# Late norms, a stationary-weight router and fill-in products in a two-block transformer kernel

## Chip, cores and metric

One core of a Trainium2 chip runs the whole kernel. The metric is the device time of one execution in microseconds (us).

## What is computed

The reference runs two blocks, one after the other, on 256 tokens of width 1024, in float32:

```
x = first_block(x, c, ...)      # 2 layers: h = rms(x)*g*(1+scale)+shift; mixer; x += g1*mix
                                #   layer 0 mixer: forgetting attention (16 heads, causal, cumulative log gates)
                                #   layer 1 mixer: latent attention (rank 768 queries, rank 256 keys and values)
                                #   each layer: x += g2 * grouped_moe(h)  (16 experts, router, best group, top 2)
x = second_block(x, ...)        # 4 layers: x += mixer(rms(x)*w); x += relu(rms(x)*w @ up)**2 @ down
                                #   mixers: retention, MoBA, differential attention, retention
# retention: q, k rotated; s = (q k^T) * decay; o = s v; o = o * rsqrt(mean(o*o) + eps); out = (silu(g) * o) @ w_out
# router: scores = sigmoid(h @ router_w)
```

The shift, scale and gate rows come from silu(c) @ w_mod (6 x 1024 columns a layer). MoBA and the differential layer add a bias that depends on the distance of key and query and is looked up in a table of 32 buckets for each head.

## The kernel before

The 256 tokens are two blocks of 128 (TB = 2); x, [128, 2, 1024], stays on the chip. Each weight is read once, in chunks of 2 MB that are two **pieces** of 1 MB. For accuracy every product is made of three: each operand is split into a high part (float32r) and a low part (the rest), and high x high, low x high and high x low are summed in PSUM. So a piece passes through four hands: SP loads it into one of three `raw` buffers in two transfers of 512 KB (line 773; it waits until VectorE has freed the buffer, line 763), ScalarE copies it to `w_high` in two halves (line 1512, which waits until TensorE is done with the piece three before, line 1508), VectorE subtracts to make `w_low` (line 1885), and TensorE multiplies. ScalarE and VectorE take pieces in program order by `feed(n)`, which stands by hand between their other work. The order on every engine is fixed by the program; semaphores order the engines.

PSUM has two pair buffers of [128, 1024] that all products take in turn (`Use`, by the parity of its number) and Y, [128, 2048], for sums over chunks. A product into a pair waits until the use two before it was emptied (`wait_free`).

**norm** (lines 1043, 1550, 1952). In the early form ScalarE squares and sums x, GpSimd makes 1/rms (lines 845 and 847), VectorE scales x to xn (line 1949), TensorE turns xn round (16 transposes, line 1039), ScalarE writes hT_high and VectorE hT_low. In the **late** form, which mlp and the two softmax layers have, TensorE turns x itself round as soon as it is updated, and 1/rms is applied to the output of the product. The two retentions, the two experts stages, the first norm and the latent norms are early.

**Start of the program.** After the first four shift and scale columns, `thin_product` makes the 16 gate logits of attention A (48 matmuls with hT as the stationary operand and 16 moving columns, lines 968 to 970), then six chunks of `a_proj` follow (`token_product`). Between them TensorE makes running sums (`cum`, lines 1410 and 1421) that ScalarE turns into the biases bias0 and bias1. The table for MoBA's bias is made here too: its inputs are loaded by SP in `needed_later`, TensorE makes it behind `a_proj[0]` (line 1428), VectorE copies it (line 2376), and ScalarE's queue writes it 128 times over to `rel_scratch` in HBM (3 MB, line 1782); it comes back with line 1851 when retention 0 is done. POOL's queue loads w_mod pieces meanwhile (line 829), VectorE sums them by rows (`mod_rows`, lines 1906 and 1909), TensorE makes columns of them behind the last a_proj (`a_mods`, line 978), and GpSimd adds the causal mask to the two biases (line 860).

**experts** (line 1195): norm, router logits by `thin_product`, sigmoid, 13 short VectorE operations to the chosen group (`here`, line 2086), `place_tokens` (ranks), the order of the groups, from which SP takes the addresses of its first expert load, `gather_tokens`, then 16 experts.

**retention** (line 1343): twelve chunks of projections (q, k, v, g), then for each of four heads `scores`, VectorE's decay product (`start`), `weigh`, ScalarE's squares, GpSimd's 1/rms and VectorE's `finish`; when all four are finished, four groups of eight transposes, then four chunks of w_out (lines 1017 to 1027).

## Time and profile before

| | us |
|---|---|
| median of 3 runs (lowest, highest) | 2863.92 (2862.45, 2864.7) |
| the profiled execution, its own time | 2860.61 |
| its span in the trace | 2858.6 |
| TensorE busy | 2522.9 (88%) |
| VectorE busy | 1691.9 (59%) |
| ScalarE busy | 1310.5 (46%) |
| GpSimd busy | 107.3 (4%) |
| mean granted TensorE clock, of full | 0.943 |

PE is TensorE, PEld its weight loads, DVE VectorE, ACT ScalarE, POOL GpSimd, SP the engine that issues most loads; a name with a small q is an engine's queue. The engines run side by side, so the shares do not add up. The order of the stages in the trace, by their starts on TensorE: first products 57.7, attention A 173, experts of layer 0 257, latent layer 708, experts of layer 1 927, retention 0 1362, mlp 0 1586, and then MoBA, mlp, differential attention, mlp, retention 1 and mlp to the end.

### The profile page before, as it was taken

What the parts mean: (1) busy time and instruction counts of PE and PEld (TensorE: products, weight loads), DVE (VectorE), ACT (ScalarE), POOL (GpSimd) and SP (SyncE); (2) the same over time, 40 slices, a digit from 0 to 9 for tenths busy, and PEclk for the clock granted to TensorE, in tenths of its full rate; (3) what the DMA queues carried; (4) which work ended last, traced back from release to release, by engine and by line L of the source; (5) the groups of instructions that cost most, each with busy time, mean ns of one, the idle gap of its engine ahead of it and who ended that gap; (6) DMA issues with size and microseconds to landing.
All of it is one profiled execution on the core that took longest, in us unless ns stands there. A gap on an engine that the chain in (4) does not pass through costs nothing.

```text
span 2858.6 us, 32694 instructions
## 1 busy us (share of the span) xinstructions
PE 2522.9 (88%) x13386; PEld 2163.3 (76%) x13386; DVE 1691.9 (59%) x1455; ACT 1310.5 (46%) x1748; POOL 107.3 (4%) x121
## 2 busy tenths in 40 slices
PE   4876999898667799998998999889997799998999
PEld 4666777786556677776886898679976699886898
DVE  5565788786555777775643555645457455643554
ACT  2351777533333566563343444444444344343443
POOL 1020000010000000000000000100000000000000
PEclk9887999999779899999899999999999999998999
DMA  7821899993431588794453555415543255462553
GB/s 266 235 74 35 287 339 333 348 323 133 166 111 64 180 307 308 269 338 150 146 193 105 197 191 177 162 60 191 190 149 118 82 192 191 153 201 98 172 188 133
DMA packets 231302, 539.89 MB, mean 189 GB/s; under 512 B 21073, under 2 KB 29809, under 8 KB 231153
## 3 DMA queue, kind: packets, MB, share of 16 engines
q1 hardware_dynamic: 209760, 471.99, 48.2%
...
q14 instruction: 44, 0.35, 0.0%
...
## 4 chain that ended last, share of the span: by engine, by line
PE 59%; DVE 18%; DMA 10%; ACT 7%; issue 3%; POOL 1%; SPq 1%; ACTq 0%; DVEq 0%
DVE w_low L1885 7%; PE pair L921 5%; PE pair L923 5%; PE pair L929 5%; PE Y L1017 5%; PE Y L1019 5%; PE Y L1027 5%; DMA raw<-in_exp_w_down 4%; ACT w_high L1512 4%; PE pair L951 3%; PE pair L952 3%; PE pair L957 3%; DMA raw<-in_exp_w_gate 3%; DVE gates L1909 2%; PE Y L1254 2%
## 5 line engine op out<-in xcount | busy, mean ns | idle before, releaser
L1885 DVE TENSOR_TENSOR w_low<-raw,w_high 128x2048 fp32r<-128x2048 f32 (+3 forms) x456 | 1033.5, 2272 | 711.9 <-ACT w_high L1512 707.4
L1512 ACT ACTIVATE w_high<-raw 128x1024 fp32r<-128x1024 f32 (+3 forms) x912 | 911.9, 1039 | 847.6 <-PE Y L1027 237.4
L921 PE MATMUL pair<-hT_high,w_high 128*128 128x256 f32 x1280 | 314.8, 286 | 13.5 <-DVE hT_low L1941 13.5
L923 PE MATMUL pair<-hT_low,w_high 128*128 128x256 f32 x1280 | 314.3, 285 | 0.0
L951 PE MATMUL pair<-w_high,hT_high 128*128 128x512 f32 (+2 forms) x644 | 256.7, 400 | 29.8 <-DVE hT_low L1966 10.7
L921 PEld LDWEIGHTS pair<-hT_high,w_high 128*128 128x128 f32 x1280 | 248.5, 194 | 16.0 <-DVE hT_low L1941 15.1
L952 PE MATMUL pair<-w_high,hT_low 128*128 128x512 f32 (+2 forms) x644 | 254.9, 397 | 0.0
L923 PEld LDWEIGHTS pair<-hT_low,w_high 128*128 128x128 f32 x1280 | 248.6, 194 | 0.9
L1019 PE MATMUL Y<-w_high,gated_low 128*128 128x512 f32 x528 | 205.8, 390 | 0.0
L1017 PE MATMUL Y<-w_high,gated_high 128*128 128x512 f32 x528 | 205.7, 390 | 0.0
L1254 PE MATMUL Y<-w_high,gated_high 128*128 128x512 f32 x320 | 134.5, 420 | 44.6 <-DVE gated_low L2179 39.7
L951 PEld LDWEIGHTS pair<-w_high,hT_high 128*128 128x128 f32 x644 | 126.5, 196 | 57.8 <-DVE hT_low L1941 11.4
L929 PE MATMUL pair<-hT_high,w_low 128*128 128x256 f32 x1280 | 166.6, 283 | 0.0
L957 PE MATMUL pair<-w_low,hT_high 128*128 128x512 f32 (+2 forms) x644 | 160.0, 389 | 5.7 <-DVE w_low L1885 5.7
L929 PEld LDWEIGHTS pair<-hT_high,w_low 128*128 128x128 f32 x1280 | 159.3, 192 | 0.0
L1210 PE MATMUL pair<-w_high,rounded 128*128 128x512 f32 x384 | 152.8, 398 | 2.8 <-DVE gated_low L2179 2.8
L1211 PE MATMUL pair<-w_high,rounded 128*128 128x512 f32 x384 | 150.5, 392 | 0.0
L952 PEld LDWEIGHTS pair<-w_high,hT_low 128*128 128x128 f32 x644 | 126.5, 196 | 25.2
L957 PEld LDWEIGHTS pair<-w_low,hT_high 128*128 128x128 f32 x644 | 120.8, 191 | 31.7 <-DVE w_low L1885 7.4
L1039 PE MATMUL pair<-squares,work 128*128 128x128 f32 x348 | 71.2, 388 | 76.7 <-DVE work L1949 30.9
L1256 PE MATMUL Y<-w_high,gated_low 128*128 128x512 f32 x320 | 131.6, 411 | 0.0
L1027 PE MATMUL Y<-w_low,gated_high 128*128 128x512 f32 x528 | 130.4, 389 | 0.0
...
## 6 DMA issues: line engine op xcount, KB each, us to landing
raw<-in_exp_w_gate SPq DMA_DIRECT2D x128, 512.0 KB, 4.8
raw<-in_exp_w_up SPq DMA_DIRECT2D x128, 512.0 KB, 5.0
raw<-in_exp_w_down SPq DMA_DIRECT2D x128, 512.0 KB, 4.8
raw<-in_w_up SPq DMA_DIRECT2D x128, 512.0 KB, 4.5
raw<-in_w_down SPq DMA_DIRECT2D x128, 512.0 KB, 4.3
...
raw<-in_ret_w_in SPq DMA_DIRECT2D x96, 512.0 KB, 4.7
raw<-in_ret_w_out SPq DMA_DIRECT2D x32, 512.0 KB, 4.0
```

What stands on the lines that cost most here:

```text
L921: nc.tensor.matmul(ps[:, f, :], high[:, k, f * P:(f + 1) * P], hT_high[:, kk, :], start=(kk == 0 and f % 2 == 0), stop=False)
L923: nc.tensor.matmul(ps[:, f, :], high[:, k, f * P:(f + 1) * P], hT_low[:, kk, :], start=False, stop=False)
L929: last = nc.tensor.matmul(ps[:, f, :], low[:, k, f * P:(f + 1) * P], hT_high[:, kk, :], start=False, stop=(kk == KD - 1 and f % 2 == 1))
L951: nc.tensor.matmul(ps[:, b, 0:n], hT_high[:, kk, bs], high[:, k, :], start=(kk == 0), stop=False)
L952: nc.tensor.matmul(ps[:, b, 0:n], hT_low[:, kk, bs], high[:, k, :], start=False, stop=False)
L957: last = nc.tensor.matmul(ps[:, b, 0:n], hT_high[:, kk, b * P:(b + 1) * P], low[:, k, :], start=False, stop=(kk == k_blocks - 1))
L1017: nc.tensor.matmul(y, high_in[:, kk, b * P:(b + 1) * P], high[:, k, ns], start=(first and kk == 0), stop=False)
L1019: nc.tensor.matmul(y, low_in[:, kk, b * P:(b + 1) * P], high[:, k, ns], start=False, stop=False)
L1027: last = nc.tensor.matmul(y, high_in[:, kk, b * P:(b + 1) * P], low[:, k, ns], start=False, stop=False)
L1254: nc.tensor.matmul(y, gated_high[:, v % 2, 2 * h + k, 0:WIN], high[:, k, ns], start=(first and k == 0), stop=False)
L1512: nc.scalar.activation(w_high[:, s % HIGH, part], raw[:, s % RAW, part], ACT.Copy).then_inc(high_ready, 1)
L1885: V.tensor_tensor(w_low[:, s % HIGH, 0:n], part, w_high[:, s % HIGH, 0:n].bitcast(F32), ALU.subtract).then_inc(low_ready, 1)
```

## The change

- **Retention** takes the late norm. The scores are multiplied by rs squared of the key's token in VectorE's decay product, the gate is scaled in ScalarE's silu (two operations a chunk instead of one), and `finish` has the product of both factors. The transposes of head h-2 are issued in the loop, ahead of `weigh(h)`. The order of VectorE's last `feed` of the projections and the first `start` is changed.
- **The router** turns x round unscaled; xn is still made, behind. The shift goes through a product of its own (16 matmuls of one broadcast column, into Y). `thin_product` has the 16 or 32 weight columns stationary and 256 token columns moving (16 matmuls), ScalarE copies the [32, 256] sum, and four matmuls turn it back and add its halves. It waits for the second half of hT_low only at k = 4. The logits are multiplied by rs and the shift row is added on VectorE. The subtraction for xn_low moves behind `here`.
- **First products.** The table of MoBA's bias leaves this stage: its loads go to ScalarE's queue behind retention 0, its matmul stands between the second and the third up product of mlp 0, its store is issued at j = 4 and its load at j = 6 of that stage. The mod products stand behind chunks 2 to 5 and write to Y. The masks are added by VectorE in quarters (`masks_of`) and GpSimd's two operations are gone.
- **keep_busy(n)** issues n matmuls of two constant [128, 128] operands whose result nothing reads: 8 in each early norm but the first, 8 behind the router's product and 8 behind the ranks, 20 before each of the two latents.

The diff, cut to its core (declarations left out, and the bodies of the moved table and lambda code, which do the same operations in another place):

```
m.nth, m.order = nth, order
-    m.norm = norm_plan(p, p.n["update"], held=True)
+    m.norm = norm_plan(p, p.n["update"], late=True, held=True, both=True)
...
     m = Phase()
+    m.rel = None
...
+        if layer == 0 and j == 2:
+            m.rel = p.fills(1)[0]
...
     r = Phase()
-    r.norm = norm_plan(p, p.n["update"])
+    r.norm = norm_plan(p, p.n["update"], late=True)
...
         p.cum.append(p.fills(1)[0] if j < 5 else None)
-        if j == 0:
-            p.rel = p.fills(1)[0]
-    p.a_mods = p.mods(4)
+    p.take("mod", 4)
...
             load_mods(STAGES["a"])
-            wait_emptied(pool, plan.cum[4])
-            for bias, mask in ((bias0, causal[:, P:S]), (bias1, causal)):
-                nc.gpsimd.tensor_tensor(bias, bias, spread(mask, 1, HEADS), ALU.add).then_inc(masked, 1)
...
-            def thin_product(use, which):
+            def thin_product(use, which, nth, other_half):
...
+                for k in range(KD):
+                    if k == KD // 2:
+                        wait_emptied(pe, other_half)
+                    both = thin_parts[:, which, k].rearrange("p i n -> p (i n)")
+                    nc.tensor.matmul(pair(use)[0:32, 0:S], both, hT_high[:, k, :], start=(k == 0), stop=False)
+                    last = nc.tensor.matmul(pair(use)[0:16, 0:S], thin_high[:, which, k, :], hT_low[:, k, :],
+                                            start=False, stop=(k == KD - 1))
+                last.then_inc(thin_summed, 1)
+                pe.wait_ge(thin_copied, nth + 1)
...
-                    bs = slice(b * P, (b + 1) * P)
-                    ps = pair(use)[:, b * 16:(b + 1) * 16]
-                    for k in range(KD):
-                        nc.tensor.matmul(ps, hT_high[:, k, bs], thin_high[:, which, k, :], start=(k == 0), stop=False)
-                        nc.tensor.matmul(ps, hT_low[:, k, bs], thin_high[:, which, k, :], start=False, stop=False)
-                        last = nc.tensor.matmul(ps, hT_high[:, k, bs], thin_low[:, which, k, :],
-                                                start=False, stop=(k == KD - 1))
+                    ps, tokens = pair(use)[:, 512 + b * 16:512 + (b + 1) * 16], thin_sums[:, b * P:(b + 1) * P]
+                    nc.tensor.matmul(ps, tokens, ident[0:32, 0:16], start=True, stop=False)
+                    last = nc.tensor.matmul(ps, tokens, ident[0:32, 16:32], start=False, stop=True)
...
+            def shift_product(m):
+                for k in range(KD):
+                    at = MOD[m.nth] + SH2 + k
+                    shift = mod[:, at:at + 1].to_broadcast([P, P])
+                    nc.tensor.matmul(Y[:, 1536:1536 + EXPERTS], shift, thin_high[:, 1, k, :].bitcast(F32), start=(k == 0), stop=False)
+                    last = nc.tensor.matmul(Y[:, 1536:1536 + EXPERTS], shift, thin_low[:, 1, k, :].bitcast(F32),
+                                            start=False, stop=(k == KD - 1))
+                last.then_inc(shift_done, 1)
...
+            def keep_busy(n):
+                for _ in range(n):
+                    nc.tensor.matmul(Y[:, 0:P], ident, upto_m, start=True, stop=True)
...
                 transposes(n.uses[1], x if n.late else xn, 4)
+                if n.after and not n.late:
+                    keep_busy(8)
...
             def experts(m):
-                wait_emptied(pe, norm(m.norm))
-                thin_product(m.router, 1)
+                other_half = norm(m.norm, lambda: shift_product(m))
+                thin_product(m.router, 1, m.nth + 1, other_half)
+                keep_busy(8)
...
+                keep_busy(8)
...
                 for j in range(FF_PARTS + 1):
+                    if j == 2 and m.rel is not None:
+                        pe.wait_ge(rel_in_loaded, 16 * N_REL)
+                        wait_free(pe, m.rel)
+                        nc.tensor.matmul(pair(m.rel)[0:16, 0:S], rel_in, onehot, start=True, stop=True).then_inc(fill_done, 1)
...
+                def turn_round(h):
+                    pe.wait_ge(r_taken, r.head + h + 1)
+                    transposes(r.oT[h], r_o, 4 * h)
...
+                    if h >= 2:
+                        turn_round(h - 2)
...
-                pe.wait_ge(r_taken, r.head + RH)
-                for j in range(4):
-                    transposes(r.oT[j], r_o, 4 * j)
+                turn_round(2)
+                turn_round(3)
...
                     last.then_inc(fill_done, 1)
-                if j == 0:
-                    pe.wait_ge(later_loaded, 16 * N_LATER)
-                    wait_free(pe, plan.rel)
-                    nc.tensor.matmul(pair(plan.rel)[0:16, 0:S], rel_in, onehot, start=True, stop=True).then_inc(fill_done, 1)
-            for mod_use in plan.a_mods:
-                modulation(mod_use)
-            wait_emptied(pe, plan.a_mods[-1][1])
+                if j >= 2:
+                    mod_product(STAGES["a"][j - 2], first_mods[j - 2]).then_inc(a_modulated, 1)
...
+            def copy_thin(use, nth):
+                se.wait_ge(thin_summed, nth + 1)
+                nc.scalar.activation(thin_sums, pair(use)[0:32, 0:S], ACT.Copy).then_inc(thin_copied, 1)
...
-                norm(m.norm, gain, MOD[layer] + SH2)
+                se.wait_ge(ffn_gain, m.nth + 1)
+                norm(m.norm, gain)
+                copy_thin(m.router, m.nth + 1)
+                se.wait_ge(logits_ready, m.nth + 1)
+                nc.scalar.activation(route[:, 0, :], route[:, 0, :], ACT.Sigmoid).then_inc(emptied[m.router.u % 2], 1)
+                se.wait_ge(scaled, TB * (m.norm.scaled + 1))
...
-                wait_full(se, m.router)
-                nc.scalar.activation(route[:, 0, :], pair(m.router)[:, 0:TB * EXPERTS],
-                                     ACT.Sigmoid).then_inc(emptied[m.router.u % 2], 1)
...
                     wait_full(se, use)
-                    nc.scalar.activation(r_g[:, :, c * 512:(c + 1) * 512], tokpair(pair(use)[:, :]),
-                                         ACT.Silu).then_inc(emptied[use.u % 2], 1)
+                    se.wait_ge(kept_ready, r.norm.kept + 1)
+                    for b in range(TB):
+                        last = nc.scalar.activation(r_g[:, b, c * 512:(c + 1) * 512], tokpair(pair(use)[:, :])[:, b, :],
+                                                    ACT.Silu, scale=rs_kept[:, b:b + 1])
+                    last.then_inc(emptied[use.u % 2], 1)
...
-                               [r_o[:, b, h * RDV:(h + 1) * RDV] for b in range(TB)], r.stat[h])
-                for j, use in enumerate(r.oT):
-                    high_of(r_blocks(j)[0], use, 4)
+                               [r_o[:, b, h * RDV:(h + 1) * RDV] for b in range(TB)], r.stat[h], scales=rs_kept)
+                    if h:
+                        high_of(r_blocks(h - 1)[0], r.oT[h - 1], 4)
+                high_of(r_blocks(3)[0], r.oT[3], 4)
...
                 ve.wait_ge(here_ready, m.nth + 1)
+                ve.wait_ge(xn_high_made, m.nth + 1)
+                V.tensor_tensor(xn_low, xn, xn_high.bitcast(F32), ALU.subtract)
...
                 wait_emptied(ve, (plan.out_a_mods, plan.out_b_mods)[layer][-1][1])
-                gain_of(FFN_G + layer * KD, MOD[layer] + SC2)
-                norm(m.norm, gain, MOD[layer] + SH2)
-                ve.wait_ge(xn_high_made, m.nth + 1)
-                V.tensor_tensor(xn_low, xn, xn_high.bitcast(F32), ALU.subtract)
+                V.scalar_tensor_tensor(gain[:], mod[:, MOD[layer] + SC2:MOD[layer] + SC2 + KD], 1.0,
+                                       cols[:, FFN_G + layer * KD:FFN_G + (layer + 1) * KD],
+                                       ALU.add, ALU.mult).then_inc(ffn_gain, 1)
+                ve.wait_ge(ffn_gain, m.nth + 1)
+                norm(m.norm, gain)
+                scale_rows(m.norm)
+                ve.wait_ge(shift_done, m.nth + 1)
+                link(V.tensor_copy(shift_row[:], Y[:, 1536:1536 + EXPERTS]))
+                wait_full(ve, m.router)
+                for b in range(TB):
+                    last = V.scalar_tensor_tensor(route[:, 0, b * EXPERTS:(b + 1) * EXPERTS],
+                                                  pair(m.router)[:, 512 + b * EXPERTS:512 + (b + 1) * EXPERTS],
+                                                  rs[:, m.norm.stat % 2, b:b + 1], shift_row[:], ALU.mult, ALU.add)
+                last.then_inc(logits_ready, 1)
...
                 norm(r.norm, cols[:, N1_G + layer * KD:N1_G + (layer + 1) * KD])
+                ve.wait_ge(rs_ready, r.norm.stat + 1)
+                of_tokens = rs[:, r.norm.stat % 2, 0:TB]
+                V.tensor_tensor(rs_squared[:], of_tokens, of_tokens, ALU.mult)
+                V.tensor_copy(rs_kept[:], of_tokens).then_inc(kept_ready, 1)
...
-                feed(2 * r.proj[11].chunk + 5)
+                feed(2 * r.proj[11].chunk + 4)
...
-                    V.tensor_tensor(sT[:, 0:S], decay[:, h, :], pair(use)[:, 0:S], ALU.mult)
-                    empties(use, V.tensor_tensor(sT[:, S:S + P], decay[:, h, 0:P], pair(use)[:, 512:512 + P], ALU.mult))
+                    V.scalar_tensor_tensor(sT[:, 0:S], pair(use)[:, 0:S], rs_squared[:, 0:1], decay[:, h, :],
+                                           ALU.mult, ALU.mult)
+                    empties(use, V.scalar_tensor_tensor(sT[:, S:S + P], pair(use)[:, 512:512 + P], rs_squared[:, 1:2],
+                                                        decay[:, h, 0:P], ALU.mult, ALU.mult))
...
+                    link(V.tensor_tensor(head_rs[:, h % 2, :], rs[:, r.stat[h] % 2, 0:TB], rs_kept[:], ALU.mult))
...
-                        last = V.scalar_tensor_tensor(r_o[:, b, vs], o[:, b, :], rs[:, r.stat[h] % 2, b:b + 1],
+                        last = V.scalar_tensor_tensor(r_o[:, b, vs], o[:, b, :], head_rs[:, h % 2, b:b + 1],
...
+                def lows(j):
+                    high_part, low_part = r_blocks(j)
+                    low_of(low_part, high_part, r.oT[j], r.high + j, 4)
...
+                    if h == 0:
+                        feed(2 * r.proj[11].chunk + 5)
+                    if h >= 2:
+                        lows(h - 2)
...
-                for j, use in enumerate(r.oT):
-                    high_part, low_part = r_blocks(j)
-                    low_of(low_part, high_part, use, r.high + j, 4)
+                lows(2)
+                lows(3)
...
+            def masks_of(j):
+                heads = slice(4 * (j - 1), 4 * j)
+                wait_emptied(ve, plan.cum[j])
+                for part in (bias0[:, heads, :], bias1[:, heads, P:S]):
+                    last = V.tensor_tensor(part, part, spread(causal[:, P:S], 1, 4), ALU.add)
+                return last
+            def taken(i):
+                ve.wait_ge(a_modulated, i + 1)
+                return add_bias(STAGES["a"][i], first_mods[i])
...
+                if j >= 3:
+                    taken(j - 3)
...
-                if j in (1, 2, 3):
-                    (rel_table, lambdas, turns)[j - 1]()
+                if j == 2:
+                    ve.wait_ge(thin_high_made, 2)
+                    V.tensor_tensor(thin_low[:, 1], thin[:, 1], thin_high[:, 1].bitcast(F32), ALU.subtract).then_inc(thin_ready, 1)
+                if j == 4:
+                    turns()
+                if j >= 2:
+                    masks_of(j - 1)
...
-            for mod_use in plan.a_mods:
-                mod_cols(mod_use)
-            ve.wait_ge(masked, TB)
+            link(taken(3))
...
+        rel_loads = [
+            (onehot, table["onehot"]),
+            (lam_in, w["diff_lambda_2"].rearrange("l i d -> l (i d)").to_broadcast([P, 256])),
...
-            se.wait_ge(rel_stored, 16)
-            rows_at = bass.AP(rel_scratch.tensor, P - 1, [[383, P], [384 * P, HEADS], [1, S]])
-            se.dma_start(relbias, rows_at).then_inc(rel_loaded, 16)
+            for dst, src in rel_loads:
+                se.dma_start(dst, src, allow_slow_non_contiguous=True).then_inc(rel_in_loaded, 16)
             mlp(plan.mlp0, 0)
...
+            def rel_step(m, j):
+                if j == 4:
+                    wait_emptied(se, m.rel)
+                    se.dma_start(rel_scratch, spread(rel_rows, 1, P)).then_inc(rel_stored, 16)
+                    se.wait_ge(lam_ready, 1)
+                    nc.scalar.activation(lam[:, 2:4], lam[:, 0:2], ACT.Exp).then_inc(lam_ready, 1)
+                elif j == 6:
+                    se.wait_ge(rel_stored, 16)
+                    rows_at = bass.AP(rel_scratch.tensor, P - 1, [[383, P], [384 * P, HEADS], [1, S]])
+                    se.dma_start(relbias, rows_at).then_inc(rel_loaded, 16)
...
             token_product(plan.kv_down, KD, KV_RANK + ROPE, norm(plan.kv_norm))
+            keep_busy(20)
             pe.wait_ge(latent_ready, 1)
```

## Rows read from the trace of the kernel before

**Rows 1.** Windows: stretch, its length, busy us and instructions of each engine, clock, DMA share, GB/s.

```profile
257.00:299.00 42.00, 30.67 (x163) 29.54 (x164) 24.28 (x63) 17.04 (x25) 0.00 (x0) 0.67 0.22 75
...
1503.40:1536.50 33.10, 24.91 (x90) 16.22 (x88) 12.79 (x20) 11.05 (x22) 3.53 (x8) 0.81 0.19 64
...
1586.00:1765.60 179.60, 179.55 (x1152) 164.13 (x1152) 94.88 (x54) 80.81 (x84) 0.88 (x2) 1.00 0.54 184
```

**Rows 2.** Timeline of PE, first products: start, length, work, idle before it and its releaser.

```profile
47.48 0.35 PE L968 MATMUL pair<-thin_high,hT_high 128*128 128x16 f32 x1 [6.38 <-DVE hT_low L1966]
...
57.71 0.77 PE L951 MATMUL pair<-w_high,hT_high 128*128 128x512 f32 x1
...
89.53 0.58 PE L1421 MATMUL pair<-squares,logs 128*128 128x128 f32 x1 [5.37 <-DVE work L2376]
...
129.03 0.79 PE L951 MATMUL pair<-w_high,hT_high 128*128 128x512 f32 x1 [7.50 <-ACT work L1562]
...
169.41 3.57 PE L978 MATMUL pair<-squares,gates 128*128 128x1 f32 x16 [9.22 <-DVE mod L1919]
173.24 3.03 PE L1039 MATMUL pair<-squares,work 128*128 128x128 f32 x13 [0.26 <-DVE mod L1919]
```

**Rows 3.** Timeline of DVE and POOL around 150 us.

```profile
144.02 4.49 DVE L1885 TENSOR_TENSOR w_low<-raw,w_high 128x2048 fp32r<-128x2048 f32 x2 [4.70 <-ACT w_high L1512]
151.20 18.08 DVE L1885 TENSOR_TENSOR w_low<-raw,w_high 128x2048 fp32r<-128x2048 f32 x3 [2.69 <-ACT w_high L1512]
...
149.36 15.57 POOL L860 TENSOR_TENSOR work<-work,masks 128x2048 f32<-128x2048 f32 x2 [38.15 <-ACT work L1800]
```

**Rows 4.** DMA queues and issues in 96 to 110 us (q10 is ACT's queue).

```profile
q10 hardware_dynamic: 935, 1.44, 90.6%
...
raw<-in_a_w_in SPq DMA_DIRECT2D x3, 512.0 KB, 24.3
```

**Rows 5.** Timeline of DVE and PE, from the last update of x to the router's ranks.

```profile
252.43 1.23 DVE L1995 TENSOR_TENSOR x<-x,work 128x1024 f32<-128x1024 f32 x1
...
256.93 0.44 PE L1039 MATMUL pair<-squares,work 128*128 128x128 f32 x1 [6.89 <-DVE work L1949]
...
264.79 0.35 PE L968 MATMUL pair<-thin_high,hT_high 128*128 128x16 f32 x1 [4.21 <-DVE hT_low L1966]
...
278.19 0.34 PE L1156 MATMUL pair<-route,squares 128*128 128x4 f32 x1 [3.02 <-DVE route L2086]
```

**Rows 6.** Timeline of PE: eight float32 matmuls, each recorded as two.

```profile
208.19 2.00 PE L1061 MATMUL pair<-squares,mod 128*128 128x128 f32 x16
```

**Rows 7.** Timeline of DVE and PE around retention 0.

```profile
1356.38 2.48 DVE L2503 SCALAR_TENSOR_TENSOR x<-x,rs,work 128x1024 f32<-128x1024 f32 x2 [2.30 <-POOL rs L847]
...
1367.40 0.55 PE L921 MATMUL pair<-hT_high,w_high 128*128 128x256 f32 x1 [1.69 <-DVE hT_low L1941]
...
1509.30 0.70 PE L1371 MATMUL Y<-work 128*128 128x512 f32 x1 [3.17 <-DVE work L2313]
...
1528.80 3.67 PE L1039 MATMUL pair<-squares,work 128*128 128x128 f32 x16 [3.86 <-DVE work L2322]
...
1536.47 0.78 PE L1017 MATMUL Y<-w_high,hT_high 128*128 128x512 f32 x1
...
1581.99 1.53 PE L1039 MATMUL pair<-squares,x 128*128 128x128 f32 x12 [0.48 <-DVE x L1992]
1586.05 0.36 PE L921 MATMUL pair<-hT_high,w_high 128*128 128x256 f32 x1 [2.52 <-DVE hT_low L1941]
```

**Rows 8.** Timeline of SP's queue and of PE in mlp 0.

```profile
1675.20 9.63 SPq L773 DMA_DIRECT2D raw<-in_w_down  x4
...
1698.83 0.40 PE L1017 MATMUL Y<-w_high,gated_high 128*128 128x512 f32 x1
```

**Rows 9.** Waits of PE in the latent layer; window of the kv_up products, PE alone.

```profile
PE pair L1447 <- DVE work L2444: 9.0, 1, 9.0
...
734.00:747.40 13.40, 13.34 (x50) 0.83 0.47 165
```

87 lines of the change are left out of this document (49 added, 38 removed).

## Prediction

> **What bounds the kernel now.** I read the windows first. In a whole mlp stage TensorE is busy 179.55 of 179.60 us, with DMA at 0.54 [rows 1]. Its 16 chunks take 179.6 / 16 = 11.2 us each, a piece 5.6. There TensorE sets the time. The stages that the change touches are different: 30.67 busy of 42.00 us at a clock of 0.67 between the last update of x and the first expert, 24.91 of 33.10 in the retention's heads [rows 1]. There a chain of short steps from engine to engine sets the time, and a step taken out of it comes off the end. The timeline of TensorE shows which step: for each gap, the reader is to see what ended it [rows 2, 5, 7].
>
> **First products, -34 us.** Before, the stage runs from the gate logits at 47.48 to attention's transposes at 173.24 [rows 2]. Its gaps have three causes.
> (a) 5.37 us until VectorE's copy L2376 [rows 2]: the table's matmul holds the pair.
> (b) 7.50 us at 129.03 [rows 2]. ScalarE's copy came late because its loads did: between 96 and 110 us nothing moved but ACT's queue, 1.44 MB in 14 us or 103 GB/s, while three weight loads took 24.3 us to land [rows 4]. That queue carries the 3 MB store of the table.
> (c) 9.22 us before 169.41 [rows 2]. Three w_low took 18.08 us, 6.0 each, where two before took 4.49, while GpSimd's masks ran for 15.57 us from 149.36 [rows 3]; VectorE then came late to the mod columns.
> All three causes leave the stage. The new one, built from rows: the thin product can start at 45.6, since it no longer waits for the second half of hT_low, 47.4; 16 matmuls of 256 columns at 0.22 us (the old ones take (57.71 - 47.48) / 48 = 0.21 [rows 2], bound by the stationary side; in mlp, matmuls of 256 columns keep 11.2 us for 96, 0.12 each, at full clock [rows 1], so 0.22 at half) end at 49.2; copy and hops 0.8; four float32 matmuls at half clock, twice the 0.25 of a pair of records [rows 6], 1.8. a_proj 0 starts at 51.9 instead of 57.71. It takes 13.5 (partly half clock, as before), then the next chunk waits for ScalarE's copy, 1.3: 66.7. Five chunks at 11.2 = 56.0; four sets of running sums, 12 float32 matmuls at 0.25 [rows 6] = 12.0; four mod products of four, 4.0; last copy 0.3. Attention starts at 139.0, so 34.2 us earlier. On VectorE a round holds two w_low, 4.6, one mod_rows, 6.1, two quarter masks of 0.7: 12.1 of TensorE's 15. POOL's and SP's loads want 4 MB in 15 us, 280 GB/s. Both fit. ScalarE's feed(HIGH) now stands behind the thin copy (49.9 instead of 45.2), in time for 51.9. SP's queue loses six small loads, POOL's two operations. Bounds: nothing less than (a) + (b) + (c) = 22, if new waits eat the rest; at most 38. Attention's 32 transposes run at half clock now (13 in 3.03, 0.23 each, against 12 in 1.53 in mlp [rows 2, 7]); with VectorE and TensorE busy up to there I take another 2 of the 3.3 us.
>
> **Router, twice, -10 us.** Last update of x at 252.43 + 1.23 = 253.66, transposes from 256.93, thin product from 264.79, ranks at 278.19 [rows 5]. New: transposes end at 256.5 at half clock; shift product, 16 float32 matmuls, 8 x 0.5 x 2 at full or half clock = 4.0 or 7.0; hT_low is done by 260.2, so it doesn't bind at half clock; thin product 3.5 (1.9 at full); copy 0.8; turning back 1.8 (1.0); logits 0.8, sigmoid 0.4. Routing starts at 270.7 at half clock, about 266.0 at full, where it now starts at 278.19 - 2.8 = 275.4. 4.7 to 9.4 gained. xn_low, 128x2048 like a w_low of 2.25 [rows 3], moves behind `here` and pushes the ranks' copy by 1.2. keep_busy(8), 2.0 at full or 3.5 at half clock [rows 6], lies in the 3.7 us until `here`; if that cover were gone it would cost itself. Net 3.5 to 8; I take 5 a stage, near half clock, since this stretch is at 0.67 [rows 1]. The first expert load hangs on the ranks, so the gain passes on.
>
> **Latents, -1 us.** keep_busy(20), 5.0 us at full clock [rows 6], fills half of a 9.0 us wait [rows 9]. The products behind lose (1 - 0.83) x 13.4 = 2.3 us to the clock [rows 9]; four such stretches bound the gain at 10. But 4 us of gap remain, and the 3.86 us gap of the retention is followed by transposes at 0.23 [rows 7], half clock. So nearly nothing; if a wait were under 5.0, the rest would be lost.
>
> **Retentions, twice, -20 us.** Norm: x is done at 1358.86 and the product starts at 1367.40, 8.5 us. A late norm takes 1586.05 - 1581.99 = 4.1 from the same point, 4.6 with transposes at half clock [rows 7]: -3.9, taken 4. Squares, 1/rms and kept factors lie beside the product; the first use of rs_kept is 45 us away. Tail: from 1503.3 to w_out's start at 1536.47, 33.1 us, 8.2 idle. New: the 3.17 us wait for the first decay product [rows 7] goes, as start(0) stands before a w_low. Following each head (scores 1.6, weigh 2.9, transposes 1.0, squares to finish 4.6 after weigh) I get TensorE work of 22 us and waits of 3.8, most of it before the last group: 25.8. So -7.3; the gap still ends in half clock and w_out starts in it, which costs 1.3 more than now: -6. The doubled silu costs 0.2 us where ScalarE waits for TensorE. Bounds: 3 (first wait only) to 8 each.
>
> **mlp 0, +12 us.** The store moves here. It is 3.15 MB at 103 GB/s [rows 4] = 30.6 us. ScalarE issues it in the middle of the fifth up product, at 1673 by the clock of before. The load issued at 1675.20 feeds the product that starts at 1698.83 [rows 8]; what was issued earlier lasts until then. If loads behind the store wait for its end, as [rows 4] show, that piece lands at 1706.5, ScalarE needs 2, TensorE starts at 1708.5: a gap of 9.7, and, as after other gaps of that size, half clock for some 5 us: 2.5. Loads behind it come in time (2.7 us a piece). The returning load, 2 MB at j = 6, has the slack of two pieces, 11 us, and more: 0. The six small loads on ACT's queue lie where ScalarE waits for the transposes; uncovered they'd cost up to 5. Bounds 0 (the store shares) to 20 (it is also slower beside reads).
> The Trainium skill, "DMA: Bandwidth & Descriptors", section on queues, rings and completion order, says that each DMA engine goes round-robin between its queue rows by packets. By that rule weights would have half the engines and mlp 0 would lose next to nothing, and the sum would be 2797. The trace disagrees: ACT's queue alone moved for 14 us [rows 4].
>
> **Sum.** 34 + 2 + 10 + 1 + 20 - 12 = 55. 2860.6 (the profiled execution's own time, span plus 2.0) - 55 = 2805.6; the median of the runs is 3.3 above that execution, so **2809**.
>
> **Rivals.**
> A. The store shares the engines with the weights in mlp 0: no gap. For it: the store leaves a tenth of the engines' time free. Against it: three loads waited 24.3 us beside it [rows 4]. 2797. Chance 0.17.
> B. The first products find a new bound: a mod load of 2 MB stands before each weight chunk and holds it 3 us a round, and VectorE's round of 12.1 grows beyond TensorE's; the stage gains the 22 of (a) to (c). 2821. Chance 0.18.
> C. The router gains nothing, as the shift product at half clock and xn_low take what the norm gives: 2819. Chance 0.1.
> D. The clock stays full from the shift product on, 9 instead of 5 a stage, and the latents get 5: 2797. Chance 0.1.
> E. Slower than before: the store's blocking of weights. Its price is its length less the 26 us that are in reserve (from 1673 to 1698.83), plus the half clock. At 103 GB/s that is 12; it decides from a length of about 90 us on, 35 GB/s, as it would if beside weight reads each packet took three times as long. Chance 0.02.
> The forecast, with errors of a few us in each term: 0.43.
> The range holds all but E and the outer parts of B and D: 2790 to 2832. A measurement tells some 0.2% (5.7 us) from no change: faster 0.97, same 0.01, slower 0.02.
>
> **What would show it.** Attention's first transposes at 139 or not; no gap over 2 us between chunks, w_low at 2.3 throughout. Router: thin product of 16 matmuls, ranks 3 to 8 us nearer to the last update. Heads of the retention in 26 us. In mlp 0 a gap of about 10 us some 113 us after its start, with only ACT's queue in the DMA, and none elsewhere. The forecast fails if that gap is missing, or if gaps of several us stand between the a_proj chunks.

## The result, and the profile after it

The changed kernel takes 2784.4 us (median of 4 runs, 2774.8 to 2788.9) beside 2864.3 for the kernel before: a ratio of 0.9726, 95% interval 0.9703 to 0.9748. That is 80 us; the forecast was 2809, 55 less than before. The direction was right, the time lies outside the forecast's range of 2790 to 2832. The profiled execution took 2783.2 us with a span of 2781.4, 77.2 less than the 2858.6 of before.

Where the 77.2 us lie is read by setting the start of the same step in the two traces side by side. A stage's gain is what the difference grew by over the stage.

```
stage (from start to start)                       forecast  measured
first products (to attention's transposes)            34      39.8
attention A to its last mod product                    2       0.0
router 0 (to the first expert's products)              5       5.0
experts 0                                              0       4.6
latents and attention B                                1       1.5
router 1                                               5       7.9
experts 1                                              0      -1.0
retention 0 (norm, heads, w_out)                      10      14.0
mlp 0                                                -12      -2.1
moba, mlp 1, diff, mlp 2                               0      -5.6
retention 1, mlp 3                                    10      13.1
sum                                                   55      77.2
```

The windows of the changed kernel, in the columns of [rows 1], for its router, the retention's heads, and mlp 0:

```profile
214.00:254.10 40.10, 35.12 (x202) 33.29 (x203) 25.26 (x73) 18.79 (x30) 0.91 (x2) 0.75 0.27 87
1440.30:1464.30 24.00, 20.59 (x89) 13.34 (x88) 14.65 (x24) 11.91 (x23) 3.55 (x8) 0.96 0.27 88
1514.30:1695.90 181.60, 181.60 (x1154) 165.27 (x1154) 95.77 (x61) 82.67 (x86) 0.89 (x2) 0.99 0.67 209
```

The heads take 24.0 us at a clock of 0.96, where they took 33.1 at 0.81 [rows 1]. In mlp 0 TensorE is busy for every one of its 181.6 us: the gap that the forecast put there is not in it. It is 2.0 longer than before, 0.6 for the table's matmul and most of the rest a first product partly at half clock.

TensorE's timeline in the first products, which answers to [rows 2]:

```profile
45.18 0.39 PE L977 MATMUL pair<-hT_high,thin_parts 128*32 128x256 f32 x1 [4.57 <-DVE hT_low L2026]
...
50.37 0.48 PE L960 MATMUL pair<-w_high,hT_high 128*128 128x512 f32 x1
...
64.20 0.50 PE L960 MATMUL pair<-w_high,hT_high 128*128 128x512 f32 x1 [1.73 <-ACT work L1602]
...
133.46 1.97 PE L1063 MATMUL pair<-squares,work 128*128 128x128 f32 x16 [0.33 <-ACT work L1602]
137.83 1.69 PE L1063 MATMUL pair<-squares,work 128*128 128x128 f32 x8 [2.40 <-ACT work L1626]
```

The thin product starts at 45.18 and attention's first transposes at 133.46, forecast 139.0. One gap is left between the chunks, 1.73 us. The transposes that follow now run at full clock, 16 in 1.97 us, but wait 2.40 us for ScalarE and then 1.06 for VectorE: attention's own chain took the 2 us that the forecast had hoped for there. VectorE's rows for the end of that stage answer to [rows 3]:

```profile
125.13 2.29 DVE L1945 TENSOR_TENSOR w_low<-raw,w_high 128x2048 fp32r<-128x2048 f32 x1 [4.10 <-ACT w_high L1551]
128.99 2.29 DVE L1945 TENSOR_TENSOR w_low<-raw,w_high 128x2048 fp32r<-128x2048 f32 x1 [1.56 <-ACT w_high L1551]
...
131.27 1.28 DVE L2501 TENSOR_TENSOR work<-work,masks 128x512 f32<-128x512 f32 x2
```

A w_low takes 2.29 us, where three took 18.08 together, and a pair of quarter masks takes 1.28.

The router, TensorE, answers to [rows 5], and the retention to [rows 7]:

```profile
214.00 3.67 PE L1063 MATMUL pair<-squares,x 128*128 128x128 f32 x16 [3.48 <-DVE mod L1979]
217.46 0.45 PE L993 MATMUL Y<-thin_parts,mod 128*128 128x16 f32 x2
...
224.15 0.40 PE L977 MATMUL pair<-hT_high,thin_parts 128*32 128x256 f32 x1
...
232.48 0.35 PE L1187 MATMUL pair<-route,squares 128*128 128x4 f32 x2 [1.56 <-DVE route L2146]
...
1305.59 0.55 PE L930 MATMUL pair<-hT_high,w_high 128*128 128x256 f32 x1 [1.69 <-DVE hT_low L2001]
...
1458.82 1.09 PE L1063 MATMUL pair<-squares,work 128*128 128x128 f32 x8 [0.38 <-DVE work L2420]
1462.68 1.97 PE L1063 MATMUL pair<-squares,work 128*128 128x128 f32 x8 [2.77 <-DVE work L2420]
1464.31 0.78 PE L1041 MATMUL Y<-w_high,hT_high 128*128 128x512 f32 x1
```

The shift product's 32 records stand from 217.46 to 224.15, 6.7 us, and the thin product right behind them: in this router the shift product, not hT_low, sets when the thin product starts. It runs at half clock here; in the second router the same 32 records take 4.06 us, at full clock for the most part. In the retention one wait of 2.77 us is left, before the last of the turns.

In mlp 0 the queues' shares of the DMA engines from 1606 to 1621 (q10 is ACT's queue, q1 SP's), with the loads' time to landing, answer to [rows 4]; under them the same two queues from 1620 to 1630, and then ScalarE's timeline and TensorE's row for the piece that was to be late:

```profile
q10 hardware_dynamic: 995, 1.53, 88.2%
q1 hardware_dynamic: 5, 0.02, 0.4%
...
raw<-in_w_down SPq DMA_DIRECT2D x3, 512.0 KB, 17.5
```

```profile
q10 hardware_dynamic: 594, 0.91, 51.9%
q1 hardware_dynamic: 521, 1.93, 47.5%
```

```profile
1601.06 0.61 ACTq L1750 DMA_DIRECT2D rel_scratch<-work  x1
...
1625.07 1.06 ACT L1551 ACTIVATE w_high<-raw 128x1024 fp32r<-128x1024 f32 x1 [10.78 <-DMA raw<-in_w_down]
1627.51 1.06 ACT L1551 ACTIVATE w_high<-raw 128x1024 fp32r<-128x1024 f32 x1 [1.39 <-DMA raw<-in_w_down]
...
1629.03 0.40 PE L1041 MATMUL Y<-w_high,gated_high 128*128 128x512 f32 x1
```

ACT's queue alone moves at first, as in [rows 4], and ScalarE waits 10.78 us for the load. From 1620.7 on the weights move beside the store. The first half of the piece (512 KB) is there at 1625 and the second at 1627.5; the product that needs them starts at 1629.03 without a wait, with half a microsecond to spare behind ScalarE's copy.

### The profile page after: what moved, and what is told of

It is laid out like the page before. It is cut to its first block, busy times and chain, and to the rows that moved or that the text cites. A ratio compares the mean times of both kernels' runs of the same rounds, so it can differ in the third digit from the quotient of the medians.

```text
span 2781.4 us, 33080 instructions
## 1 busy us (share of the span) xinstructions
PE 2528.6 (91%) x13554; PEld 2166.7 (78%) x13554; DVE 1684.2 (61%) x1485; ACT 1312.1 (47%) x1758; POOL 93.9 (3%) x119
## 4 chain that ended last, share of the span: by engine, by line
PE 66%; DVE 15%; DMA 8%; ACT 6%; issue 3%; POOL 1%; SPq 1%; ACTq 0%; DVEq 0%; POOLq 0%
DVE w_low L1945 6%; PE pair L930 6%; PE pair L932 6%; PE pair L938 6%; PE Y L1041 5%; PE Y L1043 5%; PE Y L1051 5%; PE pair L960 4%; PE pair L961 4%; PE pair L966 4%; DMA raw<-in_exp_w_down 3%; ACT w_high L1551 3%; DMA raw<-in_exp_w_gate 3%; PE pair L1243 2%; PE pair L1244 2%
## 5 line engine op out<-in xcount | busy, mean ns | idle before, releaser
L1945 DVE TENSOR_TENSOR w_low<-raw,w_high 128x2048 fp32r<-128x2048 f32 (+3 forms) x456 | 1022.2, 2247 | 686.6 <-ACT w_high L1551 681.9
L1287 PE MATMUL Y<-w_high,gated_high 128*128 128x512 f32 x320 | 133.9, 419 | 38.2 <-DVE gated_low L2251 33.1
L960 PEld LDWEIGHTS pair<-w_high,hT_high 128*128 128x128 f32 x644 | 124.7, 194 | 44.2 <-DVE hT_low L2001 11.2
L1243 PE MATMUL pair<-w_high,rounded 128*128 128x512 f32 x384 | 156.0, 406 | 2.7 <-DVE gated_low L2251 2.7
L1244 PE MATMUL pair<-w_high,rounded 128*128 128x512 f32 x384 | 153.5, 400 | 0.0
L1051 PEld LDWEIGHTS Y<-w_low,gated_high 128*128 128x128 f32 x528 | 99.1, 188 | 20.6
```

Source lines behind the costliest of these rows:

```text
L960: nc.tensor.matmul(ps[:, b, 0:n], hT_high[:, kk, bs], high[:, k, :], start=(kk == 0), stop=False)
L1051: last = nc.tensor.matmul(y, high_in[:, kk, b * P:(b + 1) * P], low[:, k, ns], start=False, stop=False)
L1243: nc.tensor.matmul(out(m, v), x_high, high[:, k, :], start=(h == 0 and k == 0), stop=False)
L1945: V.tensor_tensor(w_low[:, s % HIGH, 0:n], part, w_high[:, s % HIGH, 0:n].bitcast(F32), ALU.subtract).then_inc(low_ready, 1)
```

## The experiments

Twelve kernels ran. Where a ratio is given it is to the kernel before on the same chip (medians of 2855 to 2861 us). Three kernels (the small store, the store twice, the short rows) ran once each and are read by their traces alone. Single stages are read from each run's trace against the trace of before or of the changed kernel. The start of the same step, as a difference to the kernel before in us (the last two columns: to the changed kernel):

```
step                          after  b_rel  b_masks  b_ret  b_thin | no_busy  router_early
attention A's transposes      -39.8  -21.7   -8.0    -1.5    -7.0  |   0.1       0.4
w_out A                       -37.5  -23.2   -9.7    -3.2    -9.8  |   0.3       1.7
ranks 0                       -45.7  -22.8  -12.1    -5.6   -16.4  |  -0.6       6.2
experts 0, scatter            -49.4  -25.5  -16.3   -11.3   -23.0  |   5.0       6.5
w_out B                       -50.9  -26.8  -16.3   -12.8   -23.0  |   6.4       8.3
ranks 1                       -60.0  -26.3  -16.2   -12.8   -27.5  |  11.3      14.5
retention 0, first product    -61.8  -23.1  -16.4   -16.2   -28.6  |  13.0       9.3
retention 0, w_out            -72.2  -26.7  -16.3   -26.2   -29.8  |  13.1       7.8
mlp 0                         -71.8  -26.8  -16.3   -25.0   -29.8  |  13.1       7.8
moba                          -69.7  -25.6  -16.3   -23.5   -29.8  |  13.0       7.8
mlp 1                         -61.4  -20.0   -3.4   -25.1   -26.7  |   4.5      -0.8
end                           -77.2  -16.8   -2.7   -39.5   -26.5  |   8.8       3.5
```

Read it down a column. b_masks changes nothing after attention A, and still moves by 8 us up to w_out B and by 13 in moba: whole times of single executions carry some 10 us that no edit explains (the last section). The stage in which the edit stands is the reading.

**The table's part alone.** The pieces of the diff with rel_loads, m.rel and rel_step, on the kernel before.

```diff
-                if j == 1:
-                    wait_emptied(se, plan.rel)
-                    se.dma_start(rel_scratch, spread(rel_rows, 1, P)).then_inc(rel_stored, 16)
...
+                    if m.rel is not None:
+                        rel_step(m, j)
```

> The kernel before with the relative-bias part alone moved to mlp 0: its loads, its matmul, the table rows, the lambdas and the 3 MB store. Theory (the prediction's causes (a) and (b)): the 5.37 us and the 7.50 us gaps of the first products go, and the queue that was blocked by the store no longer delays loads: attention's first transposes at 160 to 161 instead of 173.2. In mlp 0 the changed kernel showed no gap over 1 us beside the store, so mlp 0 pays 0.6 for the matmul: about 12 us faster in all, 2849 beside 2861. Rival (the prediction's own term): a gap of about 10 us in mlp 0 when the store stands where the clock has other phases: 0 to 2 us faster. Rival 2: the 7.50 us gap was not the store's and stays: 5 us faster.

Measured: ratio 0.9937 (0.9916 to 0.9958). The first products gained 21.7 us, more than the 12.9 of the two gaps. Mlp 0 paid 1.3. The prediction's own term for mlp 0 is refuted here too, apart from the rest of the change. The gap (c) stands as it was, 9.63 us, so the three causes are separate:

```profile
147.76 3.57 PE L981 MATMUL pair<-squares,gates 128*128 128x1 f32 x16 [9.63 <-DVE mod L1930]
```

**The store alone, made small.** This tells the gap (b) from (a), and says where part of the other 9 us are. One head's rows are stored and read back for all 16, so the bias is that of one head.

```diff
-                    se.dma_start(rel_scratch, spread(rel_rows, 1, P)).then_inc(rel_stored, 16)
+                    se.dma_start(rel_scratch[0:1], spread(rel_rows[0:1], 1, P)).then_inc(rel_stored, 16)
```

> The kernel before with one head's rows of the table stored instead of 16 (192 KB instead of 3 MB), and that one read back for every head, so that diff's bias is that of one head; the table's matmul, rows and wait stay where they are. Moving the whole part took 21.7 us off the time to attention's first transposes (173.24), where the prediction had put 12.9 on its two gaps. Theory: the store is the second gap and what follows it. The 5.37 us gap stays, the 7.50 us gap goes, with it the half clock behind it (13.73 instead of 11.16) and the 1.41 us gap before the last chunk: 11 to 12 us, transposes at 161 to 163. Rival: the 7.50 us gap is the weight loads' own (POOL's 1 MB loads stand before them) and stays; then at most 3 us are gained. Rival 2: without the store the mod rows and masks on VectorE and GpSimd become the limit, and the transposes come at 168 or later.

Measured: attention's transposes at 162.25, 11.0 earlier. The 5.37 us gap stays, the chunk that began at 129.03 after 7.50 us of waiting [rows 2] starts at once:

```profile
89.01 0.80 PE L1421 MATMUL pair<-squares,logs 128*128 128x128 f32 x2 [5.37 <-DVE work L2376]
...
120.75 0.48 PE L951 MATMUL pair<-w_high,hT_high 128*128 128x512 f32 x1
```

That chunk takes 11.16 instead of 13.73 us: the gap cost itself and then 2.6 us of half clock. So the store was worth 7.5 + 2.6 and not 7.5. The same holds for (a), where the running sums behind the gap took 4.82 us and take 2.84 once it is gone. The gap of 1.41 us before the last chunk was expected to go with the store and stayed, at 1.32; it goes when the whole part moves. With 2.6 us before the first gap (an earlier start, a first chunk of 12.5 us for 13.5 and a shorter wait behind it) the other 9 us are found.

**The masks alone.**

```diff
-            for bias, mask in ((bias0, causal[:, P:S]), (bias1, causal)):
-                nc.gpsimd.tensor_tensor(bias, bias, spread(mask, 1, HEADS), ALU.add).then_inc(masked, 1)
...
+                if j >= 2:
+                    last_mask = masks_of(j - 1)
```

> The kernel before with the causal masks alone taken from GpSimd and put on VectorE, a quarter in each of the rounds 2 to 5. Theory (cause (c)): the three w_low at the end of the first products take 2.3 us each instead of 6.0, and the 9.22 us gap before the mod products shrinks to some 1 to 2 us: 7 to 9 us faster, attention's transposes at 164 to 166. Rival: the 6.0 us of the w_low are waits inside them or DMA traffic on the same memory and not GpSimd; then they stay and nothing is gained (0, at most 2 us slower for the masks' own time on VectorE).

Measured: ratio 0.9978 (0.9957 to 0.9998). In the trace each w_low takes 2.29 us and the gap shrinks from 9.22 to 3.23, not to the 1 to 2 expected; the transposes come 8.0 earlier. That VectorE was slowed by GpSimd's masks is shown: the w_low are the same instructions on the same data.

```profile
161.46 3.57 PE L975 MATMUL pair<-squares,gates 128*128 128x1 f32 x16 [3.23 <-DVE mod L1916]
```

**The thin products alone**, in the form of the diff's thin_product, for gates and routers, norms as before (the diff is that function and copy_thin).

> The kernel before with the thin products alone in their new form (the 32 columns of weights stationary, 256 tokens moving, turned back by four matmuls), for the gates and for both routers, the norms as before. Theory: gates: 48 matmuls of 10.2 us become 16 of 3.7 and a turn of 1.5, and the first chunk behind them runs at full clock (11.2 instead of 13.5): 7 us, of which part is eaten by the later gaps of that stage, which hang on loads: 3 to 7. Routers: the thin product is 10.4 us and becomes 3.3 to 3.7 plus 1.5, so 5 us each if routing follows at once. Sum 13 to 17 us faster. Rival: what the gates gain is lost at the table's matmul and at the store's gap, whose times are set by loads: 10 us faster. Rival 2 (against the new form): the clock stays low behind the shorter product and the router gains only 2 each: 5 us faster.

Measured: ratio 0.9903 (0.9877 to 0.9930). By its stages: 7.0 in the first products, 4.3 in each router (from w_out's last update to the ranks), 15.6 together, as expected; the other 11 of the profiled 26.5 stand in stages that are not touched. The ratio's interval, 20 to 35 us, lies above 15.6 too, and nothing here says why. The first chunk still took 13.9 us, partly at half clock, so the thin form does not by itself bring the clock:

```profile
51.00 0.80 PE L954 MATMUL pair<-w_high,hT_high 128*128 128x512 f32 x1
```

**The retention alone** (retention_plan late, turn_round, the scales by rs_kept).

> The kernel before with the retention part alone (late norm, turning back interleaved with the heads, the first decay step ahead of a w_low). Theory: what the two traces show, 4.0 us for the norm, 9.2 us for the heads, 0.4 to 1.3 back for a slower start of w_out, so 12 to 14 us a retention and 25 to 28 us in all. Rival (the prediction's size): 10 us each, 20 in all, the rest of what the two traces show being a clock that happened to stand higher.

Measured: ratio 0.9909 (0.9882 to 0.9936), 26 us of 2855. Per stage, 4.0 and 4.3 for the norms, 10.0 and 10.8 for the heads, 1.2 and 0.6 given back in w_out: 12.8 and 14.4. The theory of the traces holds, the forecast's 10 each was too small. The waits of TensorE in the last heads of retention 0, which are those of the changed kernel:

```profile
1501.56 1.06 PE L1041 MATMUL pair<-squares,work 128*128 128x128 f32 x8 [0.22 <-DVE work L2330]
1505.58 1.09 PE L1041 MATMUL pair<-squares,work 128*128 128x128 f32 x8 [0.38 <-DVE work L2341]
1509.44 1.09 PE L1041 MATMUL pair<-squares,work 128*128 128x128 f32 x8 [2.77 <-DVE work L2341]
```

**The store twice, and in short rows**, both on the changed kernel. They ask how near mlp 0 was to a gap.

```diff
+                    for i in range(2):
+                        se.dma_start(rel_scratch[i * HEADS:(i + 1) * HEADS], spread(rel_rows, 1, P)).then_inc(rel_stored, 16)
...
+                    for i in range(4):
+                        se.dma_start(rel_scratch[:, :, 96 * i:96 * (i + 1)], spread(rel_rows[:, 96 * i:96 * (i + 1)], 1, P)).then_inc(rel_stored, 16)
```

> The changed kernel with the 3 MB store of the table issued twice in mlp 0, the second one into scratch that nothing reads. In the changed kernel the store's queue had the DMA engines for itself from 1605.5 to about 1621 of its 34.9 us and shared them after that; the weight load issued at 1605.41 landed at 1625 and TensorE, which needs it at 1629, lost nothing. Theory 1: each store blocks the others' loads for its first 17 to 20 us. Two stores block 35 to 40 us, the load lands at 1641 to 1645, and TensorE has a gap of 12 to 18 us in mlp 0, most of it in one place; the execution is 13 to 20 us longer. Theory 2 (rival A as it was put, the engines are shared fairly): no gap above 2 us. Theory 3 (the prediction's, blocked for the whole length at 103 GB/s): 61 us blocked, a gap of 35 us or more.

> The changed kernel with the same 3 MB stored as four stores of a quarter of the columns, so in 8192 rows of 384 bytes instead of 2048 of 1536. If the blocking lasts as long as it takes to work through the rows one by one (what the 15 ns a row at 103 GB/s would mean), it is four times as long, 70 us or so, and mlp 0 gets gaps of 40 us or more. If it goes by bytes (the rate of writing memory), nothing changes: 17 to 20 us blocked and no gap above 2 us in mlp 0.

Measured, the store twice: a gap of 8.65 us in the middle of the chunk at whose start the forecast had put its 9.7, one of 1.34 behind it, and 3.6 of half clock behind the two. Mlp 0 is 12.7 longer than in the changed kernel, whose first product there was 1.3 slower. TensorE's gap, then the two issues on ScalarE's queue, ScalarE's next work, and its copy that ended the gap:

```profile
1646.48 0.80 PE L1041 MATMUL Y<-w_high,gated_high 128*128 128x512 f32 x1 [8.65 <-ACT w_high L1551]
...
1604.23 10.18 ACTq L1751 DMA_DIRECT2D rel_scratch<-work  x2
1614.44 1.28 ACT L1753 ACT_TABLE_LOAD   x1 [8.21 <-issue]
...
1645.37 1.06 ACT L1551 ACTIVATE w_high<-raw 128x1024 fp32r<-128x1024 f32 x1 [8.67 <-DMA raw<-in_w_down]
```

Short rows, 8192 for 2048 and the same bytes: one gap of 9.13, ahead of the up product before that chunk, and 1.6 of half clock; mlp 0 10.9 longer. The same rows of its trace:

```profile
1632.45 0.55 PE L930 MATMUL pair<-hT_high,w_high 128*128 128x256 f32 x1 [9.13 <-ACT w_high L1551]
...
1613.62 15.30 ACTq L1751 DMA_DIRECT2D rel_scratch<-work  x2
1628.95 1.28 ACT L1753 ACT_TABLE_LOAD   x1 [20.26 <-issue]
```

None of the theories holds, and the gaps are not what they were to measure. An issue of the store took 0.6 us of ScalarE's queue in the changed kernel; here the second store's issue took 9.5, and the four issues of short rows 22.2, until 1628.92. ScalarE does its copies in program order behind them. In the run with short rows that is the whole gap: the pieces that the up product needed had landed by 1610.5 and waited for ScalarE. The loads beside the short rows landed 9.1 and 13.5 us after their issue, sooner than the 19.6 and 21.7 of the changed kernel; ACT's queue was alone for 4 us, 1610 to 1614, and again from 1626 to 1638, when no load was out. So this run does not show that shorter rows block longer. With two stores the queue was alone for 16 us, 1608 to 1624, as with one; the second store never was, and from 1624 to 1668 the two stores had 68% of the engines' time and the weights 30%. There the gap has two causes: the late load was issued 4.6 us later, counted from the store's issue, since ScalarE and with it VectorE freed the buffer later, and it took 21.7 us to land where its counterpart took 17.5.

What is shown is that the stage stood at the edge, and that rival A's fair sharing is wrong as a mechanism for the first half of the store, though its time for mlp 0 was the right one. Why a store is alone at first and shares later, and what sets how long, stays open.

**Without the constant products.**

```diff
-                if n.after and not n.late:
-                    keep_busy(8)
...
-                keep_busy(8)
...
-            keep_busy(20)
```

> The changed kernel without its constant products (8 behind each router's thin product, 8 behind the ranks, 8 behind the transposes of the latent norms, 20 in each of the two latent waits). The prediction gave them 1 us in the latents and nothing in the routers. Theory: the latents lose 1.5 us, the routers 0 to 2 each in a lower clock for the gather and the first expert: 0 to 4 us slower. Rival 1: they only cost, on TensorE's queue in front of what is ready: up to 3 faster. Rival 2: they hold the clock for the long stages behind (experts, attention): 8 us or more slower.

Measured: ratio 0.9763 (0.9725 to 0.9800), beside 0.9712 and 0.9726 for the changed kernel: 10 to 15 us slower by the middle values, with intervals that overlap. In the trace, kv_down takes 8.14 us for 6.66, and the ranks run at half clock:

```profile
231.84 0.56 PE L1185 MATMUL pair<-route,squares 128*128 128x4 f32 x2 [3.53 <-DVE route L2140]
```

Local readings give 1.4 us in the latents, and from the last update of x to the first expert 0.7 us in router 0 and 2.0 in router 1, each set beside the router of the changed kernel whose shift product ran at the same clock. The clock of the shift product itself (6.85 us for 4.06 in router 1) stands ahead of that router's constant products and isn't theirs. Experts 0, which no edit touches, are 5.2 us longer; whether that is the missing cover, as the second rival has it, or the clock of one execution, no run tells. That the constant products are worth something is likely, how much is not settled.

**The router's norm early again** (norm_plan with held=True alone; the shift back in ScalarE's copy; no shift product; the 8 constant products behind the transposes come with the early norm).

> The changed kernel with the routers' norm done before the transposes as in the kernel before (rows scaled first, the shift in ScalarE's copy), the thin product kept in its new form; the shift product is gone with it. With the thin form alone the router gained 4.3 us at each place. Theory: the late norm is worth what is left of the router's 5 and 7.9 us: 1 to 4 us each, so 2 to 8 us slower than the changed kernel. Rival (C of the prediction): the shift product, 6.85 us at half clock and 4.06 at full, takes what the late norm gives: the same time within 2 us.

Measured: ratio 0.9762 (0.9735 to 0.9790), an interval that overlaps those of the changed kernel. From w_out's start to the ranks it is 4.5 us longer in router 0 and 6.2 in router 1. But 4.4 and 2.9 of that lie before the last update of x, where the edit changes nothing: w_out took 24.3 and 24.4 us, partly at half clock, for 22.1, and in router 0 VectorE's sums came 2.3 later. (In the second profile of the unaltered kernel the same stretch of router 0 was 2.1 longer, too.) What the edit can change begins at the last update. Its rows and those of the ranks, router 0 and router 1 without the late norm:

```profile
218.74 1.22 DVE L2054 TENSOR_TENSOR x<-x,work 128x1024 f32<-128x1024 f32 x1
238.66 0.56 PE L1187 MATMUL pair<-route,squares 128*128 128x4 f32 x2 [3.00 <-DVE route L2145]
...
882.53 1.22 DVE L2054 TENSOR_TENSOR x<-x,work 128x1024 f32<-128x1024 f32 x1
902.46 0.56 PE L1187 MATMUL pair<-route,squares 128*128 128x4 f32 x2 [0.98 <-DVE route L2145]
```

and in the changed kernel (the ranks of its router 0, at 232.48, are shown above):

```profile
212.64 1.23 DVE L2055 TENSOR_TENSOR x<-x,work 128x1024 f32<-128x1024 f32 x1
...
871.31 1.22 DVE L2055 TENSOR_TENSOR x<-x,work 128x1024 f32<-128x1024 f32 x1
887.96 0.36 PE L1187 MATMUL pair<-route,squares 128*128 128x4 f32 x2 [1.56 <-DVE route L2146]
```

From the end of the update to the ranks that is 18.7 us in both places without the late norm, and 18.6 and 15.4 with it. So the late norm gains 0.1 us where its shift product runs at half clock (6.85 us, router 0) and 3.3 where it runs at full clock (4.06, router 1). Rival C's reason, a shift product at half clock that takes what the norm gives, is what happened in the first case and not in the second. To the first expert's products the late norm is 1.4 us longer in router 0 and 3.8 shorter in router 1.

**The changed kernel again, and two that try to go on.**

```diff
-                    nc.tensor.matmul(Y[:, 1536:1536 + EXPERTS], shift, thin_high[:, 1, k, :].bitcast(F32), start=(k == 0), stop=False)
-                    last = nc.tensor.matmul(Y[:, 1536:1536 + EXPERTS], shift, thin_low[:, 1, k, :].bitcast(F32),
-                                            start=False, stop=(k == KD - 1))
+                    both = thin_parts[:, 1, k].rearrange("p i n -> p (i n)").bitcast(F32)
+                    last = nc.tensor.matmul(Y[:, 1536:1536 + 2 * EXPERTS], shift, both, start=(k == 0), stop=(k == KD - 1))
...
+                        for mod_use in between:
+                            mod_cols(mod_use)
...
+                keep_busy(9)
                 turn_round(3)
```

> The changed kernel once more, unaltered, timed beside the two that follow and the kernel before. Theory: what the clock grants differs from execution to execution by some 5 us of the whole, and the ratio comes out at 0.972 to 0.978 again. It is the base for the next two, and for what the constant products and the late norm of the router are worth (0.9763 and 0.9762 without them).

> The changed kernel with the shift product done in 8 matmuls of 32 columns instead of 16 of 16 (its time goes by the stationary side, 0.2 us a pass at full clock), the two halves added on VectorE, and the two mod columns copied between the two updates of x instead of behind them, so that the first transposes start one block earlier. Theory: the shift product falls from 6.85 and 4.06 to 3.4 and 2.1, the transposes end about 1.5 us earlier, and the ranks follow 3 to 5 us sooner after w_out's end at each place: 6 to 9 us faster than the changed kernel. Rival: hT_low is then what the thin product waits for, and each place gains 1.5 at most: 2 to 3 us faster in all.

> The same and constant products in more waits: 8 between the transposes and the product of every late norm (a 2.5 us wait, 10 places), 9 before the last turn of each retention (2.8 us). Theory: after such waits the clock falls in some executions, which costs 1.3 us at a product's start (24.5 for 23.3) and 0.4 to 1.5 at a retention's w_out; filling them is worth 0.5 to 1 us a place, so 5 to 10 us. Rival: where the wait is shorter than 2.0 us or the clock is already low, the constant products (4.0 us at half clock) hold up the product itself, and it comes out 0 to 10 us slower than the one before.

Measured: 0.9712 (0.9682 to 0.9741), 0.9704 (0.9676 to 0.9732) and 0.9703 (0.9683 to 0.9723). Locally the edits do what they should: the shift product is down to 1.96 us at full and 3.46 at half clock.

```profile
217.71 1.96 PE L994 MATMUL Y<-thin_parts,mod 128*128 128x32 f32 x16
...
221.26 0.42 PE L977 MATMUL pair<-hT_high,thin_parts 128*32 128x256 f32 x1 [0.40 <-DVE hT_low L2000]
```

From w_out A to the ranks it is 4.6 us shorter than in the changed kernel, from w_out B only 0.4; now hT_low is what the thin product waits for, as the rival said. The clock explains the difference: from the last update of x to the ranks it takes 14.0 and 14.4 us, and the changed kernel in its two profiles 18.6 and 18.5 where the shift product ran at half clock, 15.4 and 15.9 where it ran at full. So the edit gains 4 us in the one case and 1.4 to 1.8 in the other. The 0.7 to 3.0 us between the medians can't be told from no change by these intervals. More constant products add nothing that shows. The changed kernel is not measurably beaten.

## Why the prediction was wrong in size

**What failed: "mlp 0, +12 us".** The step reads: "If loads behind the store wait for its end, as [rows 4] show, that piece lands at 1706.5". [Rows 4] show 14 us in which only ACT's queue moved; I took it that the loads wait for the whole 3.15 MB, 30.6 us. The store's length was about right (34.9 us), and the blocking was real and was found again (995 of 1001 packets from 1606 to 1621). But it ends 19.6 us after the store's issue at 1601.06, and then the weights move beside the store. The piece had landed at 1627.5, 7 us before the forecast's time (1706.5 less the 71.8 by which the stage starts earlier, 1634.7), and with ScalarE's copy it was ready 27.5 us after the store's issue, where TensorE needs it after 28.0. By the forecast's sum it would have been ready after 35.5, which is where its gap of 9.7 came from. Rival E's reserve of 26 us leaves out the 5 us that the forecast's own sum gives to landing and copy behind the blocking. Mlp 0 cost 2.1, so 9.9 of the 22.2 us that the profiled pair missed are this term. The whole length of the store in the old trace would have shown it: issued at 89.51, and the first weight packets moving again at 114.6, while the store went on to 126. The other terms missed the remaining 12.3 us between them; with this term alone put right the forecast would have been 2799.

**First products, -34: right in its three causes, 5.8 too small.** (b) is shown by the small store, (c) by the masks alone, and (a) by the table's part, in which its gap goes, beside the small store, in which it stays. The new stage was mis-sized in several terms: the products before the first chunk end 1.5 us earlier than put; the first chunk was put at 13.5 us and took 11.2, but the way from it to the second chunk was 1.4 longer than put; from the second chunk on the stage took 69.3 us for 72.3, as four running sums went by at 2.6 to 2.7 us from start to start and not 3.0 each, and five chunks at 11.0 and not 11.2. The first chunk is in part luck: in the eight profiles of the changed kernel and its variants it took 11.1 to 11.2 us in four and 12.6 to 13.8 in the others, 13.8 when the changed kernel was profiled again. Rival B (a new bound) did not come. The 2 us for attention were wrong: it gained nothing. Its transposes ran at full clock, but from them to w_out the changed kernel and its variants took 50.5 us or more, the kernel before and its variants 45.5 to 48.3; the forecast had no term for that, and what beside the two waits above it hangs on was not followed. Cause (c) was also read too evenly: of the three w_low, "6.0 each", two took 4.98 and 10.98 us and the third, behind the masks, 2.28 (the last section).

**Retentions, -20: mechanism right, 7 too small.** The norm is exact, 4.0 and 4.3 for 4. The heads took 23.9 us, 25.8 were forecast: "TensorE work of 22 us and waits of 3.8". The work is 20.6 and the waits 3.4 (the window above); the transposes that move between the heads run at full clock. And w_out's slow start cost 0.4 where 1.3 were charged. Retention 0 has another 1.2 us from its projections, which no term covers.

**Routers, -10: 12.9 measured.** Router 0 is exact, 5.0; router 1 gained 7.9, as its shift product ran at full clock (4.06 for 6.85 us). Which router gets the full clock is not fixed: in the second profile of the changed kernel the shift product took 3.94 us in router 0 and 6.85 in router 1. The split by parts, from the last update of x to the ranks (24.5 us before): 4.3 for the thin form; 1.5 more in the run without the late norm, which beside that has the subtraction for xn_low behind `here` and the constant products; then 0.1 or 3.3 for the late norm by the clock of its shift product. The way from the ranks to the first expert's products is 0.9 and 1.3 longer and takes that back. Rival D's full clock is what happened in router 1, not in router 0. The forecast's routing "about 266.0" at full clock is 265.4 by its own terms.

**Latents, -1: right**, 1.5 us, and the clock was full only in kv_down.

**What no term covers**: 2 us in all over the experts and the softmax layers, made of +4.6, -1.0 and -5.6, no larger than what such stages do in kernels where nothing of them was changed.

The Trainium skill's round-robin between queue rows ("DMA: Bandwidth & Descriptors", on queues, rings and completion order) was weighed against the trace. Its time for mlp 0, next to nothing, came true; its mechanism didn't for the first half of the store, and fits the second: from 1620 to 1630 the two queues have 51.9 and 47.5% of the engines' time with 594 and 521 packets, and together move 285 GB/s.
